# First attention: the row maxima enter the scores as four contraction rows instead of through diagonal products

## What is computed

```python
    log_f = jax.nn.log_sigmoid(proj[..., 3 * hw:] + b_f)
    c = jnp.cumsum(log_f, axis=1).transpose(0, 2, 1)
    ...
        s = jnp.einsum('bqhd,bkhd->bhqk', q[:, t0:t1], k[:, :t1]) * scale
        s = s + c[:, :, t0:t1, None] - c[:, :, None, :t1]
        s = jnp.where(mask, s, -jnp.inf)
        p = jax.nn.softmax(s, axis=-1)
        outs.append(jnp.einsum('bhqk,bkhd->bqhd', p, v[:, :t1]))
```

## Time and profile before

| | |
|---|---|
| time, three runs | 1215.00, 1215.11 and 1217.24 us; median 1215.11 us |
| the profiled execution | 1215.11 us, of it a span of 1213.2 us from the first to the last instruction |
| busy share of the span | PE 97%, DVE 46%, ACT 41%, POOL 46% |
| chain that ended last | PE 73%, issue 14%, POOL 7%, DVE 4%, ACT 2% |
| TensorE's mean granted clock | 0.994 of full speed |

### The profile page before, as it was taken

One profiled execution on the slowest core, in us unless ns is written; L12 is line 12 of the kernel. 1 busy time (PEld: TensorE's weight loads), 2 busy tenths in 40 slices (PEclk: granted clock), 3 DMA queues, 4 the chain that ended last, 5 costly groups with the idle time before them and its releaser, 6 DMA issues.

```text
span 1213.2 us, 15111 instructions
## 1 busy us (share of the span) xinstructions
PE 1179.3 (97%) x5634; PEld 981.9 (81%) x5634; DVE 558.6 (46%) x701; ACT 499.1 (41%) x665; POOL 561.3 (46%) x389
## 2 busy tenths in 40 slices
PE   6999999989999999999999999989999999999998
PEld 6887878877888888888888788877888888888887
DVE  5857878876643100233222788856633100243000
ACT  4348778864322211222233688854322211222121
POOL 4523533524665544555544443324565544555442
PEclk9999999989999999999999999989999999999999
DMA  6321121122233335333233211112233333233331
GB/s 215 96 70 35 35 69 35 35 70 70 70 104 104 104 92 151 104 104 96 78 104 104 70 35 36 35 35 70 69 104 104 104 104 89 84 104 104 104 104 35
DMA packets 142237, 101.22 MB, mean 83 GB/s; under 512 B 3128, under 2 KB 141552, under 8 KB 142192
## 3 DMA queue, kind: packets, MB, share of 16 engines
q1 hardware_dynamic: 142128, 100.56, 28.1%
q10 hardware_dynamic: 64, 0.03, 0.0%
HBM read 98.47 MB, written 2.12 MB: 83 GB/s over the span
## 4 chain that ended last, share of the span: by engine, by line
PE 73%; issue 14%; POOL 7%; DVE 4%; ACT 2%; DMA 1%; SPq 0%; POOLq 0%; ACTq 0%; DVEq 0%
PE ps L1258 22%; PE ps L1260 22%; PE ps L1259 22%; POOL w_lo L414 4%; POOL fox_sq_lo L421 2%; PE ps L1618 2%; DVE xn_lo L901 1%; DVE rst L873 1%; DVE x_hat L894 1%; ACT w_hi L486 1%; DMA x_in<-in_x 1%; POOL w_lo L457 1%; PE ps L1581 0%; PE ps L1600 0%; PE ps L1603 0%
## 5 line engine op out<-in xcount | busy, mean ns | idle before, releaser
L414 POOL TENSOR_TENSOR w_lo<-stage,w_hi 128x512 fp32r<-128x512 f32 x344 | 503.3, 1493 | 463.4 <-ACT w_hi L486 456.3
L486 ACT ACTIVATE w_hi<-stage 128x2048 fp32r<-128x2048 f32 x88 | 168.5, 1914 | 475.3 <-PE ps L1260 470.3
L1258 PE MATMUL ps<-xn_hi,w_hi 128*128 128x512 f32 x720 | 285.0, 396 | 0.3 <-issue 0.3
L1260 PE MATMUL ps<-xn_hi,w_lo 128*128 128x512 f32 x720 | 280.5, 390 | 0.0
L1259 PE MATMUL ps<-xn_lo,w_hi 128*128 128x512 f32 x720 | 280.2, 389 | 0.0
L1258 PE MATMUL ps<-r_hi,w_hi 128*128 128x512 f32 x512 | 199.8, 390 | 0.0
L1260 PE MATMUL ps<-r_hi,w_lo 128*128 128x512 f32 x512 | 199.3, 389 | 0.0
L1259 PE MATMUL ps<-r_lo,w_hi 128*128 128x512 f32 x512 | 199.2, 389 | 0.0
L1258 PEld LDWEIGHTS ps<-xn_hi,w_hi 128*128 128x128 f32 x720 | 135.2, 188 | 30.5 <-issue 2.6
L1259 PEld LDWEIGHTS ps<-xn_lo,w_hi 128*128 128x128 f32 x720 | 135.2, 188 | 29.1 <-issue 1.9
L1260 PEld LDWEIGHTS ps<-xn_hi,w_lo 128*128 128x128 f32 x720 | 135.1, 188 | 28.5
(11 more groups left out here) (208 smaller groups left out, 1642.0 us busy)
## 6 DMA issues: line engine op xcount, KB each, us to landing
stage<-in_w_up SPq DMA_DIRECT2D x32, 1024.0 KB, 5.4
stage<-in_w_down SPq DMA_DIRECT2D x32, 1024.0 KB, 5.5
stage<-in_w_in_a SPq DMA_DIRECT2D x16, 512.0 KB, 5.0
stage<-in_w_in_a SPq DMA_DIRECT2D x4, 1024.0 KB, 6.2
stage<-in_w_out_a SPq DMA_DIRECT2D x4, 1024.0 KB, 5.0
stage<-in_w_q_b SPq DMA_DIRECT2D x4, 1024.0 KB, 5.0
stage<-in_w_out_b SPq DMA_DIRECT2D x4, 1024.0 KB, 4.9
x_in<-in_x SPq DMA_DIRECT2D x4, 512.0 KB, 7.5
```

Of the source, the lines that this page charges most:

```text
L414: ins = nc.gpsimd.tensor_tensor(w_lo[:, s, c], stage[:, s, c], w_hi[:, s, c].bitcast(F32), ALU.subtract)
L486: nc.scalar.activation(w_hi[:, s, :], stage[:, s, :], ACT.Copy).then_inc(w_hi_ready, 1)
L1258: mm(out_, st_hi, mv_hi, start=start, stop=False)
L1260: return mm(out_, st_lo, mv_hi, start=False, stop=stop)
```

## The change

- `C_ROW = 16`: the gate's 16 rows are moved from partitions 0 to 15 to 16 to 31 (weights `wf`, bias `bf`, `pick`), so that partitions 0 to 3 of `c_split` are free. They get ones, and `pick` gets ones there too: on the key side of `qk_hi` four rows now hold 1.
- On the query side the same four rows are set to zero once, after the ones were written, and `ones_ready` is posted a third time after that; the first `proj_pair` waits for three.
- `fox_max` no longer makes `diag`. It adds `nm` to a running `fox_shift`, 128x4 a head (the earlier pair's shift is still in the four rows when the approximate scores are formed, so `nm` is the rest). Then, for both heads, it waits until TensorE has turned the shift into four rows (`fox_turn`) and spreads these over the four query blocks in `qk_hi` (4x512, from the bank and the identity).
- `fox_turn(j, e)` is one matmul of 128 columns with a 4-column stationary operand, into the bank from which the maximum was reduced. It stands in `proj_pair` of the keys ahead of chunk 5 for head 0 and of chunk 7 for head 1; for the last pair both stand together ahead of `fox_scores(7)`.
- `fox_scores` loses the product with `diag`: four matmuls a head.

```diff
+        fox_shift = sb("fox_shift", [P, 2, TB], F32R)
-        diag = at("diag", [P, 2, T], F32R, area + 46 * KB)
...
+        C_ROW = 16
...
+            V.tensor_scalar(fox_shift[:].rearrange("p e b -> p (e b)"), ident[:, 0:2 * TB], 0.0, None, ALU.mult)
+            dve.wait_ge(constants_ready, 4)
+            V.memset(pick[0:TB, :], 1.0)
             V.memset(vx[:, :, HD:2 * HD], 1.0).then_inc(ones_ready, 1)
...
+            ins.then_inc(ones_ready, 1)
+            dve.wait_ge(ones_ready, 2)
+            for e in range(2):
+                rows = slice(64 - 64 * e, 64 - 64 * e + TB)
+                ins = V.tensor_scalar(qk_hi[rows, 0, e, :].rearrange("p (b n) -> p b n", b=TB),
+                                      ctemp[rows, None, C_ONES - C_TEMP:C_ONES - C_TEMP + P].to_broadcast([TB, TB, P]),
+                                      0.0, None, ALU.mult)
             ins.then_inc(ones_ready, 1)
...
+            V.tensor_copy(c_split[0:TB, :], ct[0:TB, 3, :]).then_inc(gate_vector_step, 1)
+            dve.wait_ge(gate_vector_step, 6)
...
-                    after(dve, fox_scores_done, 2 * j - 1 + e)
-                    V.tensor_tensor(diag[:, e, :].rearrange("p (b n) -> p b n", b=TB),
-                                    ident[:, None, :].to_broadcast([P, TB, P]),
-                                    nm[:, e, :, None].to_broadcast([P, TB, P]), ALU.mult).then_inc(fox_diag_ready, 1)
+                    V.tensor_tensor(fox_shift[:, e, :], fox_shift[:, e, :].bitcast(F32), nm[:, e, :], ALU.add
+                                    ).then_inc(fox_shift_ready, 1)
+                for e in range(2):
+                    dve.wait_ge(fox_shift_turned, 2 * j + e + 1)
+                    rows = slice(64 - 64 * e, 64 - 64 * e + TB)
+                    V.tensor_tensor(qk_hi[rows, 0, e, :].rearrange("p (b n) -> p b n", b=TB),
+                                    ps[0:TB, SCORE_BANKS[e][0], None, 0:P].to_broadcast([TB, TB, P]),
+                                    ident[0:TB, 0:TB, None].to_broadcast([TB, TB, P]), ALU.mult).then_inc(fox_rows_ready, 1)
...
+                    if turn_before is not None and k >= KC - 3 and k != KC - 2:
+                        fox_turn(turn_before, k // (KC - 1))
...
+            def fox_turn(j, e):
+                pe.wait_ge(fox_shift_ready, 2 * j + e + 1)
+                mm(ps[0:TB, SCORE_BANKS[e][0], 0:P], fox_shift[:, e, :], ident_r[:], start=True, stop=True
+                   ).then_inc(fox_shift_turned, 1)
...
-                    pe.wait_ge(fox_diag_ready, 2 * j + e + 1)
+                    pe.wait_ge(fox_rows_ready, 2 * j + e + 1)
...
-                        mm(o, ones_r[:], diag[:, e, qs], start=False, stop=False)
...
-            pe.wait_ge(ones_ready, 2)
+            pe.wait_ge(ones_ready, 3)
```

More of the change, by code:

```diff
@@ L253, in build @@
         fox_max_ready = sem("fox_max_ready")
-        fox_diag_ready = sem("fox_diag_ready")
+        fox_shift_ready = sem("fox_shift_ready")
+        fox_shift_turned = sem("fox_shift_turned")
+        fox_rows_ready = sem("fox_rows_ready")
         fox_scores_done = sem("fox_scores_done")
@@ L347, in _ @@
                     sp.wait_ge(wf_zero, 2)
-                    sp.dma_start(bf[0:HEADS, :], b_f[0].rearrange("(h o) -> h o", o=1)).then_inc(wf_landed, 16)
-                    sp.dma_start(wf[:, :, 0:HEADS], w_in[:, :, 3 * D:3 * D + HEADS]).then_inc(wf_landed, 16)
+                    sp.dma_start(bf[C_ROW:C_ROW + HEADS, :], b_f[0].rearrange("(h o) -> h o", o=1)).then_inc(wf_landed, 16)
+                    sp.dma_start(wf[:, :, C_ROW:C_ROW + HEADS], w_in[:, :, 3 * D:3 * D + HEADS]).then_inc(wf_landed, 16)
             def load_pair(i, s):
@@ L942, in _ @@
                 V.tensor_copy(dst[:], src)
-            V.tensor_tensor(pick[:], ident[0:64, 0:HEADS], ident[0:64, 32:32 + HEADS], ALU.add)
+            V.tensor_tensor(pick[:], ident[0:64, C_ROW:C_ROW + HEADS], ident[0:64, 32 + C_ROW:32 + C_ROW + HEADS], ALU.add
+                            ).then_inc(constants_ready, 1)
+            V.tensor_scalar(fox_shift[:].rearrange("p e b -> p (e b)"), ident[:, 0:2 * TB], 0.0, None, ALU.mult)
+            dve.wait_ge(constants_ready, 4)
+            V.memset(pick[0:TB, :], 1.0)
             V.memset(vx[:, :, HD:2 * HD], 1.0).then_inc(ones_ready, 1)
@@ L1023, in fox_max @@
                     dve.wait_ge(fox_max_scores_done, 2 * j + e + 1)
-                    after(dve, fox_diag_ready, 2 * j - 1 + e)
+                    after(dve, fox_shift_ready, 2 * j - 1 + e)
                     b0, b1, b2 = SCORE_BANKS[e]
@@ L1328, in _, with proj_pair @@
             pe.wait_ge(v_stored, 4)
-            def proj_pair(i, s, t, sum_before=None):
+            def proj_pair(i, s, t, sum_before=None, turn_before=None):
                 if t == 0:
@@ L1415, in fox_step @@
                 fox_max_scores(i - 1)
-                proj_pair(i, s, 1, (i, 0))
+                proj_pair(i, s, 1, (i, 0), i - 1)
                 fox_scores(i - 1)
@@ L1502, in _ @@
             out_piece(0, 0, both, range(3, 5))
+            fox_turn(PAIRS - 1, 0)
+            fox_turn(PAIRS - 1, 1)
             fox_scores(PAIRS - 1)
```

## The result

| | before | after |
|---|---|---|
| median of the runs | 1215.05 us (1214.18 to 1217.24, 4 runs) | 1231.95 us (1229.88 to 1233.85, 4 runs) |
| profiled execution, its span | 1215.11 us, 1213.2 us | 1230.4 us, 1228.4 us |

The ratio of after to before is 1.0135, with a 95% interval from 1.0117 to 1.0154. The changed kernel is slower by 17 us. The forecast was 5 us more, with an upper end of 1223.5 us: the sign was right, the time fell outside the range.

A forecast was written before the change was run, and what follows sets the result against it. TensorE, busy 97% of the span, was taken as the bound, with GpSimd also pacing the first attention's steps. Terms 0.2 + 2.9 + 2.8 - 0.9 - 2.0 + 1.5 + 0.4 = +4.9 us gave 1220.0 us, range 1211.5 to 1223.5 us.

The forecast's parts named there:

- The copy's +0.2: Ahead of the values' copy, two small instructions and a wait enter VectorE's queue: +0.2 us (0.1 to 0.4).
- The zeroed rows: Before the first projection, two 4x512 TENSOR_SCALAR take turns with GpSimd's w_lo and delay TensorE: +2.9 us.
- Rival B: Zeroed rows don't collide with GpSimd: they take 1.0 us, the clock stays, 1215.3 us; chance 0.17.
- The clock: Idleness before the first projection brings the clock to 1.2 GHz from 76.0 to 82.8: +2.8 us (0 to 3.4).
- rival A: No low clock at the start, the clock holds through the idle time: 1217.2 us; chance 0.13.
- Step 1: First attention: TensorE reaches the sum at 105.95, GpSimd is there by then without two diag collisions: -0.9 us.
- Steps 2 and 4: First kind, VectorE ahead of GpSimd: without diag the sum comes at about 129.0 instead of 130.09, together -2.0 us.
- Steps 3, 5, 6: GpSimd first: additions wait for w_lo, TensorE waits 1.3 us for the second turn; +0.5 us each, +1.5 us together.
- Step 7: First attention: GpSimd there waits for ScalarE, which has more to do before the keys' squares: 0.
- Last pair: Scores start 2.7 us later as additions wait for w_lo; less product and low-clock work come back: +0.4 us.
- Rival C: 128x4 additions don't collide with w_lo: 1210.3 us with B's start, 1215.0 us with the forecast's; chance 0.16.
- Rival D: Waits in the steps bring the clock down, 3.4 us for each of three steps: 1230 us; chance 0.04.

The follow-up runs named there:

- run 5: Changed kernel with the overlaid tiles 512 bytes from their old place (area = cursor[0] + 480): 1218.44 us, ratio 1.0017 to the kernel before.
- run 1: Changed kernel with the overlaid tiles 64 bytes from their old place (area = cursor[0] + 32): 1223.86 us, ratio 1.0073 to the kernel before.
- run 4: Changed kernel, overlaid tiles as in run 1, the four rows zeroed inside the cast by a factor per partition: 1220.38 us, ratio 1.0034 to the kernel before.
- run 9: Changed kernel, rows zeroed inside the cast, overlaid tiles 512 bytes from their old place, addition left where the change put it: 1214.85 us, ratio 0.9999 to before.
- Run 8: Changed kernel, rows zeroed in the cast, overlaid tiles 512 bytes off, maxima in nm_r turned by a second product, addition deferred: 1208.95 us, ratio 0.9943 to before.
- run 3: Kernel before with all tiles moved 32 bytes alike: 1216.68 us, ratio 1.0012 to the kernel before.
- run 6: Kernel before with the weights w_hi and w_lo moved 32 bytes and everything behind them 64: 1239.23 us in one run.
- run 7: Kernel before with the overlaid tiles moved 256 bytes: 1217.18 us in one run.
- run 10: Kernel before with xn_hi and xn_lo alone moved 32 bytes, everything behind them 64 bytes: 1227.73 us in one run.
- run 11: Kernel before with the overlaid tiles moved 128 bytes: 1225.46 us in one run.
- run 2: Kernel before with the overlaid tiles moved 32 bytes and nothing else: 1230.3 us, ratio 1.0129 to the kernel before.

## Why the prediction was wrong, step by step

**The step that failed is the sum.** "0.2 + 2.9 + 2.8 - 0.9 - 2.0 + 1.5 + 0.4 = +4.9 us" holds a term for each edit that executes, and none for the declaration of a tile, `fox_shift`, ahead of `area`. That term is +12.7 us by the products' spacing, of the 13.1 us that arise behind 271 us in the profiled execution, and 13.5 us between the medians of after and of 5. The diff showed the line; the sum should have had an entry "the overlaid tiles move by 32 bytes", and since no row of before showed what that does, a bound. Even then its size could only have been learned from a run.

Without it the profiled execution would have been at 1215.1 + 2.1 = 1217.2 us, inside the range. Its 2.1 us are made up so, by the prediction's terms:

- *Ahead of the attention.* VectorE's casts of the ones end 0.45 us earlier in this execution than before (73.76 against 74.22 us); why isn't shown. No term stood for that. The copy's +0.2 can't be told apart from it.
- *The zeroed rows*, 2.9: measured 2.78 us for the pair, and 3.03 us of idleness where 3.2 were forecast. Right. Rival B (1.0 us) has fallen: beside the `w_lo`, four partitions (2.78 us) take as long as 64 (2.87 us). The Trainium skill (SBUF — State Buffer, Who interferes with whom) names `tensor_scalar` among the operations that can take the port pair shared with GpSimd; the trace agrees, 1.39 us for one of 4x512 beside `w_lo`, against 0.99 us for two of 64x512 with GpSimd idle.
- *The clock*, 2.8: low from 75.65 for 6.8 us, as forecast (76.0 for 6.8 us). The first approximate scores start at 99.20 instead of 94.09 us; 5.11 + 0.45 - 2.81 leaves 2.75 us, where 2.81 is what the zeroed rows moved the first projection by. Right in this execution, and in part by luck: with the same instructions the clock didn't fall there at all in the profiled execution of run 1 (rival A came true in it), and was low for 3.4 us in that of run 5. Nor did taking the zeroed rows away bring back 2.9 + 2.8 us: it brought 3.5 us (4.7 by the ratios) in 4 against 1, and 0.18%, 2.2 us (at most 4.6 by the intervals), in 9 against 5. How often the clock falls there these runs don't show.
- *Step 1*, -0.9: measured 111.48 - 99.20 against 106.88 - 94.09, -0.5. `fox_sq_lo` was still 0.30 us late.
- *Steps 2 and 4*, -2.0: measured -1.3 and -1.5, together -2.8. I had GpSimd bound them at 129.0, with TensorE at 128.9; it was TensorE alone, which had no wait left at the sum. *Steps 3, 5, 6*, +1.5: measured +0.2, +0.2 and -0.9, together -0.5. The wait for the second turn was there, in 3 and 5, but 0.83 us instead of 1.3: its end was right (3.9 us behind the start of `w_lo` forecast, 152.30 - 148.50 = 3.8 measured), but TensorE came to it later, since the first turn, at 149.87, had already come 0.23 us late. The term stood at +0.5 a step and measured +0.2. Step 6 turned into one of the first kind. *Step 7*, 0: measured 0.0. Taken together -3.7 us for steps 1 to 7 where I had -1.4: of the work that executes this is the term that was mis-sized most, and most of the reason why 2.1 us were left of the 4.9.
- *Last pair*, +0.4: from the last sum to the first product of pT 24.70 instead of 24.06 us, +0.6. Right, with two waits of 2.2 us in place of one of 2.9.

Rival C, that additions of 128x4 slip in beside GpSimd, has fallen by the 1.28 us of the addition in step 3. Rival D, that these waits bring the clock down, didn't happen in the steps.

That step 6 changed its kind is more than an error of rounding. Whether a step has the wait hangs on whether VectorE's addition starts 0.09 us ahead of `w_lo` or 0.03 behind; the wait stood in steps 3 and 5 of after and of run 9, in 3, 4 and 5 of runs 1 and 5, and in 3, 5 and 6 of run 4. A step with it is 1.1 us longer than one without. Run 8 has no such wait in any step.

## What to carry to other kernels

When a diff adds or resizes a tile, write down which tiles move against which, and compare the mean duration of a group of products that the diff doesn't touch: a change of 6 ns in 1900 products outweighed all that the change was about. Tiles that are operands of the same product belong on fixed places, with padding in front, so that a small tile can come and go. A small operation of VectorE that another engine waits for should not be one that takes turns with GpSimd: let TensorE add the two parts itself, and do the addition where nobody waits.

## What the runs showed of the hardware

In these runs the start-to-start time of 512-column fp32r products depends on the distance in SBUF between the stationary and the moving operand: 226.7 ns at the place of before and 256 or 512 bytes from it, 233.3 ns at 32 and 128 bytes, between 226.0 and 231.7 at 64; the same shift of both costs nothing (1.0012, 0.9998 to 1.0025). The rows can't show the mechanism; that reads of weights and of the moving operand meet is a guess. The Trainium skill (SBUF — State Buffer, Who interferes with whom) gives TensorE two independent read ports and says that it never waits on anyone. No run here shows it held up at a port by another engine, but the products of runs 3 and 6 differ by 6.6 ns through the place of their operands alone.

Behind the first 15 us of the span the stretches at 1.2 GHz lasted 3.4 or 6.8 us wherever they appeared (at 57 to 59, 76 to 78, 98, 258 to 266, 693 and 783 to 806 us in different executions). The same wait of TensorE brought the clock down in some profiled executions and not in others:

| wait | clock fell | clock stayed |
|---|---|---|
| for `v_all`, 2.2 to 2.6 us | runs 1, 3, 4, 6, 7, 9, 10, 11 | before, after, runs 2, 5, 8 |
| for `diag` in the last pair, 2.8 to 3.0 us | before, runs 3, 6, 7, 10 | runs 2, 11 |
| for the zeroed rows, 3.0 to 3.2 us | after, run 5 | run 1 |

So the length of a wait of 2.2 to 3.2 us didn't tell whether the clock would fall. The fall in run 4 at 98 us, behind a wait of 1.2 us, is in none of the rows.
